# Gate sums from 16-bit one-hot matrices, and three-pass expert blocks beside them, in a two-layer hybrid model with product-key experts

## The reference, cut to what matters

```
def expert_block(args):
    xb, ib, gb = args
    a = jnp.einsum('thkd,td->thk', down[ib], xb).astype(jnp.float32)
    c = (gb * jax.nn.gelu(a)).astype(up.dtype)
    return jnp.einsum('thk,thkd->td', c, up[ib]).astype(x.dtype)
```

## Time and profile before

| | |
|---|---|
| median of three runs | 2859.25 us (2859.18 to 2859.89) |
| span of the profiled execution | 2858.0 us; what lies around it is the difference to a run's time, 1.25 us to the median |
| TensorE busy | 2840.0 us, 99% of the span |
| VectorE busy | 1988.3 us, 70% |
| ScalarE busy | 1511.6 us, 53% |
| GpSimd busy | 113.5 us, 4% |
| granted TensorE clock | 0.999 of full over the whole span |
| act stage beside the gates, layer 0 | block 14 begins at 269.28 us, block 31 ends at 421.6 us |

### The profile page before, as it was taken

One profiled execution on the slowest core, in us unless ns is written; L12 is line 12 of the kernel. 1 busy time (PEld: TensorE's weight loads), 2 busy tenths in 40 slices (PEclk: granted clock), 3 DMA queues, 4 the chain that ended last, 5 costly groups with the idle time before them and its releaser, 6 DMA issues.

```text
span 2858.0 us, 44352 instructions
## 1 busy us (share of the span) xinstructions
PE 2840.0 (99%) x17542; PEld 2542.5 (89%) x17542; DVE 1988.3 (70%) x3010; ACT 1511.6 (53%) x2219; POOL 113.5 (4%) x81
## 2 busy tenths in 40 slices
PE   8999999999999999999999999999999999999998
PEld 7899988889999899999888999988899988888997
DVE  7889999655555788999966555566655556665664
ACT  6644874544444575488454444445455444545543
POOL 0033000000000002400000000000000000000000
PEclk9999999999999999999999999999999999999999
DMA  6344556765554534455676554556555656554663
GB/s 215 119 163 164 195 190 204 278 250 179 178 201 164 177 111 163 142 209 181 214 280 243 191 191 176 187 179 185 182 166 180 188 187 185 170 184 155 176 186 133
DMA packets 223376, 530.13 MB, mean 185 GB/s; under 512 B 13514, under 2 KB 87408, under 8 KB 211952
## 3 DMA queue, kind: packets, MB, share of 16 engines
q1 hardware_dynamic: 221872, 521.11, 54.8%
q0 software_dynamic: 1344, 6.82, 0.7%
HBM read 507.81 MB, written 20.06 MB: 185 GB/s over the span
## 4 chain that ended last, share of the span: by engine, by line
PE 98%; DVE 1%; DMA 0%; issue 0%; ACT 0%; SPq 0%; DVEq 0%
PE ps L2650 16%; PE ps L2632 13%; PE ps L1518 13%; PE ps L1528 12%; PE ps L1506 12%; PE ps L1446 9%; PE ps L1463 5%; PE ps L602 4%; PE ps L593 4%; PE ps L1435 2%; PE ps L2909 2%; PE ps L1236 1%; PE ps L2818 0%; PE ps L2802 0%; PE ps L1348 0%; DMA common_sb<-in_common 0%
## 5 line engine op out<-in xcount | busy, mean ns | idle before, releaser
L2251 DVE TENSOR_TENSOR ring_lo<-ring,w_hi 128x1024 fp32r<-128x1024 f32 x320 | 388.4, 1224 | 242.9 <-ACT w_hi L2247 241.7
L2247 ACT ACTIVATE w_hi<-ring 128x1024 fp32r<-128x1024 f32 x320 | 335.2, 1056 | 235.4 <-PE ps L2650 168.7
L1518 PE MATMUL ps<-h_t_lo,down_hi 128*128 128x256 f32 x1024 | 288.2, 281 | 0.0
L1518 PE MATMUL ps<-h_t_expert,down_lo 128*128 128x256 f32 x1024 | 287.8, 281 | 0.0
L1518 PE MATMUL ps<-h_t_expert,down_hi 128*128 128x256 f32 x1024 | 286.8, 280 | 0.0
L1446 PE MATMUL ps<-h_t,ring 128*128 128x256 f32 x1216 | 283.5, 379 | 0.0
L2632 PE MATMUL ps<-h_t_lo,w_hi 128*128 128x256 f32 x928 | 260.7, 281 | 0.0
L2632 PE MATMUL ps<-h_t_hi,w_hi 128*128 128x256 f32 x928 | 259.4, 280 | 0.1
L2632 PE MATMUL ps<-h_t_hi,ring_lo 128*128 128x256 f32 x928 | 259.0, 279 | 0.0
L1446 PEld LDWEIGHTS ps<-h_t,ring 128*128 128x128 f32 x1216 | 221.1, 190 | 24.9
L1122 ACT ACTIVATE out_hi<-ring 128x1024 fp32r<-128x1024 f32 x128 | 135.6, 1060 | 159.2 <-PE ps L1506 153.1
(11 more groups left out here) (522 smaller groups left out, 7225.2 us busy)
## 6 DMA issues: line engine op xcount, KB each, us to landing
ring<-in_peer_down SPq DMA_DIRECT2D x128, 1024.0 KB, 5.1
ring<-in_w_in SPq DMA_DIRECT2D x140, 512.0 KB, 3.7
ring<-in_peer_up SPq DMA_DIRECT2D x68, 1024.0 KB, 4.8
ring<-in_w SPq DMA_DIRECT2D x132, 512.0 KB, 3.7
ring<-in_peer_up SPq DMA_DIRECT2D x120, 512.0 KB, 4.3
late_gates<-arena SPq DMA_DIRECT2D x64, 256.0 KB, 4.2
arena<-late_gates SPq DMA_DIRECT2D x16, 1024.0 KB, 6.9
ring<-in_w_out SPq DMA_DIRECT2D x16, 512.0 KB, 3.9
```

Of the source, the lines that this page charges most:

```text
L1518: m = pe.e.matmul(PS[:, 4 + b, j * T:(j + 1) * T], w[:, b, o], x[:, kc, :], start=kc == 0 and n == 0, stop=kc == KD - 1 and n == 2)
L2247: a.e.activation(W_HI[:, g % HI_SLOTS, :], RAW[:, g % RAW_SLOTS, :], ACT.Copy).then_inc(*a.count(f"c{g}_hi"))
L2251: v.e.tensor_tensor(RAW_LO[:, g % RAW_SLOTS, :], RAW[:, g % RAW_SLOTS, :], W_HI[:, g % HI_SLOTS, :].bitcast(F32), ALU.subtract).then_inc(* ...
```

## The change

1. **Gates in 16-bit floating point.** `hot_first`, `hot_mask`, both halves of `hot_second`, the indices and the gate parts become fp16. The gate is multiplied by 2^14, split in two fp16 parts, and the copy out of PSUM scales back. VectorE makes all four tensors of a group (each 128x1024, fp16 in and out, with the inner pair of elements adjacent); ScalarE's eight ACTIVATEs per group go. `sums(s)` is two matmuls of 128 columns per token that accumulate in the same place, eight in all. The sums take one PSUM bank, in turn of four, and ScalarE's `gates_out` alone takes them to the gates; `gates_low` goes.
2. **Blocks 16 to 31 in three passes.** ScalarE splits the halves (`lead_high`, in between its gate copies, one for each group), VectorE does the low part of half 0 behind `hot(n)` of every even n, GpSimd that of half 1. The high parts go to slots in turn (`turn_slot`). Loads and places stay as they were. From block 18 on the input is the pair `h_t_expert`, `h_t_lo`, which are now made early: `ht_hi` by ScalarE at block 5, `ht_lo` by VectorE behind `hot(1)`.
3. **The second `up` block** is loaded in two halves during block 31 and not during block 17, since its place now holds high parts; its slots in the out stage are renumbered.

```
-            for n in range(GROUPS_OF_TOKENS + 1):
...
+            lead_high(a, LEAD + 1, (1,))
+            lead_high(a, FIRST_TURN, (0,))
+            for s in range(SUMS):
+                gates_out(s)
+                if s < SUMS - 1:
+                    acts_out(s)
+                n = s // 2 + 1
+                if s % 2 == 0 and n < 2 * (HELD - FIRST_TURN):
+                    lead_high(a, FIRST_TURN + n // 2, (n % 2,))
...
+                for b in range(FIRST_TURN, HELD):
+                    lead_low(p, b, 1)
...
                 for j in range(FEW):
-                    k, at = s % 2 * FEW + j, j % 2 * T
-                    m = pe.e.matmul(PS[:, bank + j // 2, at:at + T], HOT1[:, n % 2, k, :],
-                                    HOT2[n % 2][:, k, :, :].rearrange("p i n -> p (i n)"), start=True, stop=True)
+                    k = s % 2 * FEW + j
+                    for part in range(2):
+                        m = pe.e.matmul(PS[:, GATE_BANKS[s % banks], j * P:(j + 1) * P], HOT1[:, n % 2, k, :],
+                                        HOT2[n % 2][:, k, part, :], start=part == 0, stop=part == 1)
...
-                if b == 0 or b in LEAD_SPLIT or b in GATE_SPLIT:
+                if b == 0 or b in LEAD_SPLIT or b >= LEAD:
+                    if b == OWN_X and q == 0:
+                        pe.e.wait_ge(*pe.at("ht_lo"))
                     passes_quarter(b, q)
...
+                v.e.tensor_tensor(paired(MASK[:, n % 2, :, :]), pairs, each(HK_SECOND[:, at:at + GROUP, :]), ALU.is_equal) \
+                    .then_inc(*v.count(f"mask{n}"))
                 if n >= 2:
                     v.e.wait_ge(*v.at(f"sum{2 * n - 3}"))
+                v.e.tensor_tensor(paired(HOT1[:, n % 2, :, :]), pairs, each(HK_FIRST[:, at:at + GROUP, :]), ALU.is_equal) \
                     .then_inc(*v.count())
                 v.e.wait_ge(*v.at(f"mask{n}"))
+                for part in range(2):
+                    v.e.tensor_tensor(paired(HOT2[n % 2][:, :, part, :]), paired(MASK[:, n % 2, :, :]),
+                                      each(PARTS[:, part, at:at + GROUP, :]), ALU.mult) \
+                        .then_inc(*v.count(f"hot_low{n}" if part else None))
...
                 hot(n)
                 if n == 0:
                     lead_low(v, LEAD + 1, 1)
+                if n == 1:
+                    v.e.wait_ge(*v.at("ht_hi"))
+                    v.e.wait_ge(*v.at(f"act_mm{max(b for b in range(1, LEAD) if b not in LEAD_SPLIT)}"))
+                    v.e.tensor_tensor(HT_LO[:, :, :], HT[:, :, :], HT_EXPERT[:, :, :].bitcast(F32), ALU.subtract) \
+                        .then_inc(*v.count("ht_lo"))
+                if n % 2 == 0:
+                    lead_low(v, FIRST_TURN + n // 2, 0)
```

More of the change, by code:

```diff
@@ L14 @@
 U32 = mybir.dt.uint32
[L15 removed]
+F16 = mybir.dt.float16
 I32 = mybir.dt.int32
@@ L606, in front_chunk, with turn_of, turn_slot, turn_free @@
                 pe.mark(f"h{j}_mm")
+        def turn_of(b, j):
+            return 2 * (b - FIRST_TURN) + j
+        def turn_slot(n):
+            if n == 1:
+                return GATE_HI1[:, :]
+            return (RAW_LO[:, 6, :], RAW_LO[:, 7, :], OUT_LO[:, 1, :])[(n - 2) % 3 if n else 2]
+        def turn_free(n):
+            if n == 0:
+                last = max(2 * i + j for i in range(len(LEAD_SPLIT)) for j in range(2) if (2 * i + j) % LEAD_SLOTS == 1)
+                return f"act_half{LEAD_SPLIT[last // 2]}{last % 2}"
+            if n == 1:
+                return f"act_half{LEAD}1"
+            if n < 4:
+                return f"act_mm{max(i for i in LEAD_LOADS if LEAD_PLACE[i] == (1, 1))}"
+            n -= 4 if n == 4 else 3
+            return f"act_half{FIRST_TURN + n // 2}{n % 2}"
         def lead_slot(b, j):
+            if b >= FIRST_TURN:
+                return turn_slot(turn_of(b, j))
             if b == 0:
@@ L686, in gates_of, with gate_sums @@
                            ap=[whole.ap[0], [late - early, 2], [64, FEW], [1, 64]])
[L688 to L692, removed]
+        def gate_sums(s):
+            return PS[:, GATE_BANKS[s % len(GATE_BANKS)], :].rearrange("p (k h n) -> p h k n", k=FEW, h=2)
         def raw(which, slot):
@@ L1069, in hybrid_scalar, with gates_out @@
                     a.e.activation(BESTV, OFF, ACT.Exp).then_inc(*a.count("best_exp"))
[L1071 to L1082, removed]
+            def gates_out(s):
                 if s // 2 >= STAGES and s % 2 == 0:
@@ L1959, in hybrid_vector @@
             choice_gates(v)
-            def gates_low(s):
-                v.e.wait_ge(*v.at(f"high{s}"))
-                v.e.tensor_tensor(gates_of(s), gate_sums(s, 1), gates_of(s), ALU.add).then_inc(*v.count(f"low{s}"))
             def hot(n):
                 at = n * GROUP
-                numbers = IOTA.unsqueeze(1).broadcast_to([P, GROUP, P])
-                halves = NUMBERS[:, :].rearrange("p (a b) -> p a b", b=2).unsqueeze(1).broadcast_to([P, GROUP, P // 2, 2])
-                second = HK_SECOND[:, at:at + GROUP, :].unsqueeze(2).broadcast_to([P, GROUP, P // 2, 2])
+                pairs = NUMBERS[:, :].rearrange("p (a b) -> p a b", b=2).unsqueeze(1).broadcast_to([P, GROUP, P // 2, 2])
@@ L2005, in hybrid_vector @@
                     lead_low(v, LEAD + 1, 1)
-            for s in range(SUMS - 4, SUMS):
-                gates_low(s)
-            v.e.wait_ge(*v.mine())
+                if n == 1:
+                    v.e.wait_ge(*v.at("ht_hi"))
[4 more added lines that the diff above has]
+                    lead_low(v, FIRST_TURN + n // 2, 0)
+            v.e.wait_ge(*v.at(f"gates{SUMS - 1}"))
             fold(0, 1)
@@ L3273, in _ @@
                     if b == len(LEAD_LOADS) + 1:
[L3274 to L3277 removed]
+                        last = max(i for i in LEAD_LOADS if LEAD_PLACE[i] == (0, 1))
+                        sp.e.wait_ge(*sp.at(f"act_mm{last}"))
+                        peer_block(sp, "up", 0, 0, l, "up_in0")
+                    if b == HELD:
+                        for j in range(2):
+                            sp.e.wait_ge(*sp.at(f"act_half{HELD - 2 + j}{1 - j}"))
+                            held_up(sp, l, 1, j, f"dma_w{6 + j}")
                     i = b - 2 - LEAD
                     for n in range(LATE_BY[i - 1] if i > 0 else 0, LATE_BY[i] if i >= 0 else 0):
[L3280 removed]
+                        sp.e.wait_ge(*sp.at(f"gates{2 * n + 1}"))
                         sp.e.dma_start(late_gates[:, n * GROUP * 64:(n + 1) * GROUP * 64], ARENA[:, late_stage(n):late_stage(n) + GROUP * 64]) \
```

101 lines of the change are left out of this document (40 added, 61 removed).

## The result

The changed kernel takes 2939.55 us, median of four runs (2939.08 to 2940.90), against 2859.57 for the kernel before in runs beside it (2859.18 to 2861.72): ratio 1.0278 (95% interval [1.0266, 1.029]), 80 us slower. Forecast was 2910 with 2922 as upper end, so the direction held and the size did not: 80 where 51 stood. One profiled execution has a span of 2937.5 us.

What follows compares the result with a forecast made beforehand. TensorE, busy 99% of the span, bounded the kernel; after the change, waits behind each load would. Start +5.8, block 16 +1.9, fourteen blocks +19.0, block 31 -1.2 make +25.5 a layer, +51 in all: 2910 us, range 2860 to 2922.

Steps and rivals of the forecast that it cites:

- TensorE's own work, 16 us a layer on offer: Stage of blocks: if TensorE never waited, 136.2 us a layer instead of 152.3.
- P: TensorE's work after the last matmul of block b - 2: four sums at 0.52, four quarters at 1.43, 7.8 us.
- C = 12.5: Last matmul of block b - 2 to sums ahead of block b: landing, high part, low part, fp16 group, GpSimd's 2.40.
- GpSimd gets in between two VectorE operations and holds them out: GpSimd's low part of half 1 shuts out a VectorE operation for its full 2.40 us in each block.
- rival 1: VectorE keeps the port, GpSimd works mostly in VectorE's wait for a landing: about +12.5 us a layer, 2884; chance 0.24.
- Rival 2: No contention between two-input operations of VectorE and GpSimd: +4 us a layer, 2867, or 2855 with faster landings; chance 0.2.
- fp16 operations at 0.68: VectorE's four fp16 operations per group go at the bf16 mask's rate, 0.68 us, 2.5 for four.
- rival 4: 16-bit VectorE operations take 1.22 us each, not the mask's rate: +66 us a layer, 2991; chance 0.04.
- Two blocks take C + P: Blocks 17 to 30: a pair takes at least chain plus one block's work, 20.3 us with GpSimd's exclusion, against 17.58.
- E(k): End of block k, taken as the time the sums ahead of it go, plus P.
- The terms, layer 0: Per layer: start +5.8, block 16 +1.9, fourteen blocks 17 to 30 +19.0, block 31 -1.2, together +25.5 us.
- Rival 3: Load lands in under 2.9 us, so TensorE bounds, two blocks 15.6 us: 2831; chance 0.1.

Runs made afterwards that it cites:

- the best version: Changed kernel with both low parts on VectorE behind the odd group and loads of blocks 18 to 31 cut in two halves: 2832.08 us, ratio 0.9902.

## Why the prediction was right in kind and too small

- **TensorE's own work, 16 us a layer on offer.** Right, with some luck. P was 7.8 and is 7.76; the best version collects 27.7 us of about 32. But two misses cancel in P: eight sums measure 0.43, below the 0.47 that was the lower bound and the 0.52 that was taken, and the quarter behind them 1.51 (7.76 / 4 - 0.43), not 1.43. The Trainium skill's 81 ns for each (TensorE: Matmul & The Clock Gate, section Back-to-back issue gap), an estimate of 0.65 for eight, does not fit this trace, which has 54 (64 with the longer matmul behind them).
- **C = 12.5.** Right. Load issue to sums is 12.16 to 12.91, mean 12.38 over seven; the landings had a median of 5.5 against 5.2.
- **GpSimd gets in between two VectorE operations and holds them out.** Right, and rival 1 fell for all but one block a layer: GpSimd's subtraction took 2.38 to 2.67, hardly stretched, and an fp16 operation up to 2.83. The exception is block 17, where VectorE never paused and GpSimd's took 4.95 and 4.81; it cost nothing there. Rival 2 fell: taking the reader out gives 51 us. Its own price of 2867 was too low as well: the two kernels without GpSimd's reads take 2887 to 2889, since the clock falls behind their idles too.
- **fp16 operations at 0.68.** Right; rival 4 fell.
- **Two blocks take C + P.** The law held and what was put into it for E(k) did not. The idle was to be 20.3 - 15.6 = 4.7 us, and is 4.4 to 5.2 in the pairs. But pairs take 21.6 to 23.4, not 20.3, since P behind an idle is not 7.8. Without what the clock takes they are at 20.3.
- **The terms, layer 0.** The start came to +5.8, as forecast (sums ahead of block 16 at 287.51 against 281.72). Block 16 came to +0.8 (9.42 against 8.61), not +1.9, and 1.7 of its 9.42 are the clock's: `ht_lo` and the low part of block 17 held up nothing. The fourteen blocks came to +34.1 (157.2 against 123.1), not +19.0, and 14.9 of that are the clock's. Block 31 came to -1.2, as forecast.
- **The step that failed: P was taken at full clock after a stop of TensorE.** Nothing in the sum priced it, and the range's upper end held none of it. The earlier trace rows show a clock digit of 9 in all 40 slices; before, TensorE had no idle of 4 us in this stage, so no row there could show what follows one. After each of the eight idles of a layer the next block lost 1.4 to 2.8 us, 16.6 us in layer 0 and 16.2 in layer 1, 33 in all. That is more than the 29 us by which the forecast was short, because block 16 had been put too high. Filling the idles with idle work takes 31 us off and lands near the forecast.
- **Late `up` block, stores, out stage: nothing.** Right to within 1.5 us.
- **Rival 3, 2831.** It fell as a forecast for this kernel, since the landing was 5.5 and not 2.9. Its price fits what a kernel takes that TensorE bounds: the best version takes 2832, though by another way than an early landing. What it missed is that the chain can be shortened at another place than the landing. The prediction saw that VectorE sat in its wait with hot(2i + 1) behind it, and did not ask what the same instructions cost in another order.

Where the 80 us go, by the single edits: moving one line gives 92 back, cutting the load 81, leaving the load out 79, taking GpSimd's reads out 51, keeping TensorE at work 31. Together they are far more than the loss, because each shortens the same chain or lifts the same clock penalty. Behind the chain stands the joint work of VectorE and GpSimd (8.15 to 8.4 a block), and only behind that TensorE (7.76).

Open: which idles lose the clock. In all of these kernels the idles of 4.0 us and more in this stage always did. For shorter ones the length does not decide: with both low parts on VectorE an idle of 1.94 us lost it and one of 3.30 did not. Three-pass blocks beside the old 32-bit gates were not tried, and it was not looked into why some landings take 6 us.

## What to carry to other kernels

Behind a wait on a slow event, count everything that the engine has queued there and who needs it: the same operations in the order "what others wait for first, the wait last" were worth 92 us in this kernel, 33 of them the clock's. Where two buffers alternate and the load waits for the place, two blocks take at least the chain from release to use plus one block's work; give back the place in halves, or shorten the chain, and compare with twice the work. An idle of TensorE of 4 us is to be priced with the slow matmuls behind it (here 2.1 us each in the mean). Work given to GpSimd that reads SBUF is to be priced as if its full duration were taken from VectorE, where VectorE's operations have two inputs as here (28 of 32 subtractions shut one out).

## What the runs showed of the hardware that was not expected

- After an idle of 4.4 to 5.5 us TensorE ran partly at 1.2 GHz: granted clock 0.53 over 3.6 us behind one of them, 0.21 us for a matmul that else takes 0.12. A block lost 1.4 to 1.8 us behind half of these idles and 2.5 to 2.8 behind the others.
- Eight 16-bit products of 128 columns with a weight load each take 0.43 us in a row, 54 ns each, less than four 32-bit ones of 256 columns (0.47); yet the matmul behind them takes 0.20 and not 0.12, and a half-group is longer than before beside three-pass blocks (1.94 against 1.89) and beside plain ones (by 0.03). Why the matmul behind takes longer stays open.
- Three writes by GpSimd to SBUF in 2.97 us left VectorE's two-input operations at 0.69 us; one subtraction of 2.4 to 2.7 us stretched one to 2.83. It goes the other way too: where VectorE had no pause, GpSimd's subtraction took 4.95.
- Time in which VectorE and GpSimd wait for each other is shown as busy: VectorE at 30.70 of 31.00 us, GpSimd at 4.72 for a subtraction that alone takes 2.40.
